# Two ways to take the inverse roots of thirteen RMS norms: square root plus reciprocal, or logarithm plus exponential

## The reference: what is computed

```python
def rms_norm(x, g):
    x32 = x.astype(jnp.float32)
    y = x32 * lax.rsqrt(jnp.mean(x32 * x32, axis=-1, keepdims=True) + RMS_EPS)
    return (y * g.astype(jnp.float32)).astype(x.dtype)
```

## Time and profile before

| | |
|---|---|
| median of three runs | 3220.3 us |
| profiled execution, its own time | 3220.06 us |
| its span (first to last instruction) | 3217.5 us |
| PE busy | 3034.4 us (94%) |
| DVE busy | 1767.5 us (55%) |
| ACT busy | 1015.8 us (32%) |
| mean granted clock of PE | 0.967 |

### The profile page before, as it was taken

How to read it: one execution, slowest core, us unless ns; L and a number is a source line. 1 busy time by engine, 2 the same in 40 slices (tenths; PEclk the granted TensorE clock), 3 DMA queues, 4 the chain that set the end, 5 groups by cost and what they waited for, 6 DMA issues and landing times.

```text
span 3217.5 us, 51830 instructions
## 1 busy us (share of the span) xinstructions
PE 3034.4 (94%) x21724; PEld 2586.9 (80%) x21724; DVE 1767.5 (55%) x3317; ACT 1015.8 (32%) x1745; POOL 222.6 (7%) x455
## 2 busy tenths in 40 slices
PE   8999999999999899999999999989999897789997
PEld 7777998999999887789897888858888464568886
DVE  4564577457566447457755756556356453553334
ACT  4655232332122246523223222233222215332221
POOL 0130222000000102122200000000000000000000
PEclk8989999999999999989999999989999998899998
DMA  5201111235443320111123545312334210122231
GB/s 176 101 15 47 50 67 59 71 135 181 144 137 112 119 79 28 47 45 64 59 80 138 183 145 170 117 49 98 110 114 172 102 32 29 53 70 102 90 100 70
DMA packets 74494, 302.47 MB, mean 94 GB/s; under 512 B 10728, under 2 KB 11112, under 8 KB 69272
## 3 DMA queue, kind: packets, MB, share of 16 engines
q1 hardware_dynamic: 57880, 230.04, 21.1%
q0 software_dynamic: 16384, 69.13, 6.0%
HBM read 288.51 MB, written 14.63 MB: 94 GB/s over the span
## 4 chain that ended last, share of the span: by engine, by line
PE 85%; DVE 7%; ACT 5%; issue 2%; DMA 1%; POOL 0%; ACTq 0%; DVEq 0%; SPq 0%
PE acc L1040 17%; PE acc L1041 17%; PE acc L1042 17%; PE acc L1302 5%; PE acc L1303 5%; PE acc L1304 5%; PE acc L1059 2%; PE acc L1205 2%; ACT temps L1709 1%; PE acc L1074 1%; DVE work L2035 1%; PE acc L1179 1%; PE acc L1533 1%; PE acc L1152 1%; PE acc L1347 1%
## 5 line engine op out<-in xcount | busy, mean ns | idle before, releaser
L1041 PE MATMUL acc<-normed_r,toep_r 128*128 128x512 f32 (+1 forms) x1824 | 642.8, 352 | 0.0
L1638 ACT ACTIVATE toep_r<-ring 128x1024 fp32r<-128x1024 f32 (+2 forms) x340 | 392.6, 1157 | 707.4 <-PE acc L1042 691.1
L2086 DVE TENSOR_TENSOR ring_r<-ring,toep_r 128x1024 fp32r<-128x1024 f32 (+2 forms) x340 | 457.9, 1348 | 261.6 <-ACT toep_r L1638 261.2
L1041 PEld LDWEIGHTS acc<-normed_r,toep_r 128*128 128x128 f32 x1824 | 344.5, 189 | 46.1 <-issue 0.2
L1040 PE MATMUL acc<-mixed_r,toep_r 128*128 128x264 f32 (+1 forms) x1056 | 342.6, 324 | 5.1 <-DVE ring_r L2086 4.4
L1040 PE MATMUL acc<-work_r,toep_r 128*128 128x512 f32 (+1 forms) x988 | 341.7, 346 | 1.5 <-DVE ring_r L2086 1.4
L1042 PE MATMUL acc<-work_r,ring_r 128*128 128x512 f32 (+1 forms) x988 | 340.9, 345 | 0.0
L1042 PE MATMUL acc<-mixed_r,ring_r 128*128 128x264 f32 (+1 forms) x1056 | 338.8, 321 | 0.0
L1040 PE MATMUL acc<-temps_r,toep_r 128*128 128x512 f32 x768 | 305.0, 397 | 24.3 <-DVE normed_r L2072 14.8
L1041 PE MATMUL acc<-work_r,toep_r 128*128 128x512 f32 (+1 forms) x880 | 307.3, 349 | 0.0
L1302 PE MATMUL acc<-residual_r,toep_r 128*128 128x264 f32 (+1 forms) x1024 | 301.8, 295 | 3.7 <-ACT toep L1818 2.1
(11 more groups left out here) (408 smaller groups left out, 5379.3 us busy)
## 6 DMA issues: line engine op xcount, KB each, us to landing
ring<-in_w_pair SPq DMA_DIRECT2D x176, 512.0 KB, 3.5
ring<-in_w_down SPq DMA_DIRECT2D x64, 704.0 KB, 4.1
ring<-in_w_gb SPq DMA_DIRECT2D x64, 640.0 KB, 3.9
extra<-in_w_ada POOLq DMA_DIRECT2D x18, 1024.0 KB, 6.2
toep<-in_w_ada POOLq DMA_DIRECT2D x18, 1024.0 KB, 6.1
ring<-in_w_tm SPq DMA_DIRECT2D x24, 512.0 KB, 4.5
ring<-in_w_out SPq DMA_DIRECT2D x24, 512.0 KB, 3.5
ring<-in_w_fm SPq DMA_DIRECT2D x20, 512.0 KB, 3.8
```

Source lines behind the costliest of these rows:

```text
L1041: mm(out, wh, xl[:, a:z], start=False, stop=False)
L1638: A(high(ld), slot(ld), ACT.Copy).then_inc(S["w_high"], 1)
L2086: V.tensor_tensor(low(ld), slot(ld), high(ld), ALU.subtract).then_inc(S["w_low"], 1)
```

## The change

The reciprocal on VectorE and its semaphore go. `root` takes the logarithm of the mean (with epsilon as bias) and then the exponential of minus half of it, both on ScalarE; the exponential waits for the logarithm through a semaphore of ScalarE's own, and it is the exponential that releases VectorE. A new helper, `log_table`, takes the logarithm of a column of ones, which makes the logarithm's table the one in place, and it waits for its own end in the same way. It stands ahead of the squares of a norm, ahead of the last products of a feed-forward (the second half of the `down` loop), or ahead of the output products of a mixer; `n_ssm` has none.

```diff
             def root(n, rinv_used=None):
                 act.wait_ge(S["sq_used"], n["sq0"] + len(n["tiles"]))
                 if rinv_used:
                     wait(act, rinv_used)
-                A(two(RINV, n["pieces"]), n["acc"], ACT.Sqrt, bias=epsc).then_inc(S["mean_read"], 1)
-
-            def squares(n, rinv_used=None):
+                x = two(RINV, n["pieces"])
+                link(A(x, n["acc"], ACT.Ln, bias=epsc))
+                A(x, x, ACT.Exp, scale=-0.5).then_inc(S["mean_read"], 1)
+
+            chain = [0]
+
+            def link(ins_):
+
+                chain[0] += 1
+                ins_.then_inc(S["scalar_chain"], 1)
+                act.wait_ge(S["scalar_chain"], chain[0])
+
+            def log_table():
+
+                link(A(logc, onecol, ACT.Ln))
+
+            def squares(n, rinv_used=None, ahead=True):
+                if ahead:
+                    log_table()
                 for i in range(len(n["tiles"])):
                     square(n, i)
                 root(n, rinv_used)
...
+                    if half:
+                        log_table()
                     for i, j in enumerate(f["down"][half]):
...
                     high_weights(ly["out"][1].loads[0])
+                    log_table()
                     for i, j in enumerate(ly["out"]):
...
                 squares(b2["n_attn"])
-                squares(b2["n_ssm"], b2["n_attn"]["done"][-1])
+                squares(b2["n_ssm"], b2["n_attn"]["done"][-1], ahead=False)
                 high_tiles(b2["x_out"])
+                log_table()
                 for i, j in enumerate(b2["out"]):
...
             def rinv(n):
                 dve.wait_ge(S["mean_read"], n["n"] + 1)
-                r = two(RINV, n["pieces"])
-                V.reciprocal(r, r).then_inc(S["rinv_ready"], 1)
-                dve.wait_ge(S["rinv_ready"], n["n"] + 1)
                 return n["pieces"][0][0], n["pieces"][-1][1]
```

More of the change, by code:

```diff
@@ L319, in build @@
         ostat = cell(20)
+        logc = cell(1)
         dec = [cell(2) for _ in range(2)]
@@ L448, in build @@
             constants_set start_used lb_shift lb_exp lam_dots lam_exp cact_ready""".split()
-        names += """sq_ready sq_used mean_read rinv_ready stat_ready stat_rooted gate_scaled silu_ready""".split()
+        names += """sq_ready sq_used mean_read stat_ready stat_rooted gate_scaled silu_ready""".split()
         names += """u_ready h_done f_done fm_ready tm_ready gate_ready act_ready
```

## The result

The changed kernel took 3200.62 us (median of 4 runs, 3200.07 to 3202.03), the kernel before in the same timing (a set of runs taken together) 3220.53: ratio 0.9939, 95% interval [0.9922, 0.9956]. The profiled execution has a span of 3198.0 us against 3217.5, so its gain is 19.5.

The account below looks back on a forecast made before the run. TensorE was taken as the bound (85% of the chain of waits), gaining only where it waits for ScalarE and VectorE. Terms 8.7 + 2.45 + 0.6 + 1.5 + 1.9 - 2.3 = 12.85 us gave 3207.2 us, range 3201.5 to 3213.5.

Parts of the forecast that it names:

- The chain's price: At one norm, from the logarithm's start to the first normed tile: 2.66 us in place of 4.11, gain 1.45 us.
- The first norm: Program's first norm: first load ahead of the input, shorter chain, but weight splits on ScalarE behind it; gain 1.5 us.
- The clock's part of the pair: At `n_attn` and `n_ssm`: longer idle time puts the second set of means at the low clock, losing up to 2.7 us.
- The chain of one norm: Clean chains at `pre1`, `post1`, `premix`, `postmix`, `pre2`, `post2`: 1.45 us won at each, 8.7 us together.
- Second layer's first norm: There the square root's load ran late and the logarithm's table is in place long before: gain 2.45 us.
- the feed-forwards: Norms ahead of the two feed-forwards: the SiLU and the split weights come earlier; gains 1.0 and 0.9, together 1.9 us.
- the final norm: Final norm: first normed tile 1.45 us earlier, but ScalarE is late for the squares of `pre1`; gain 0.6 us.
- the early gains are swallowed: Rival: first two layers' gains (5.85 us) go into the next wait for weights or their split; 3213.0 us, chance 0.09.
- the clock gives half of them back: Rival: low-clock stretches end when they ended before, so 5.9 us is given back; 3213.1 us, chance 0.13.
- `n_attn` and `n_ssm` (-2.3): Both norms together: later squares and means, and a second set of means at the low clock; loss 2.3 us.
- I save no such stretch: Behind longer idle times elsewhere: low-clock stretches start and end earlier with the work, so no gain from the clock.

Follow-up runs that it names:

- the two later traces: Traces of the unedited changed kernel, timed twice more: 3206.56 us, ratio 0.9966, and 3203.51 us, ratio 0.9953, to the kernel before.
- the rows with one load and with two: With two: the changed kernel plus a small square root between each logarithm and its exponential, 3222.63 us; with one: the changed kernel, 3200.62 us.
- the three traces: Traces of the same changed kernel from its first timing and two later ones: 3200.62, 3206.56 and 3203.51 us.
- the late load: The changed kernel without the small logarithm ahead of the squares of `n_attn`: 3202.87 us, ratio 0.9951 to the kernel before.
- one activation: The kernel before with the reciprocal square root of the magnitude in place of square root and reciprocal, loads staying where they were: 3170.31 us, ratio 0.9857.

## Why the prediction was right, and where it failed

The chain's price was right. Three steps failed. The first norm was put at 1.5 us and gave 5.70 in the result. The clock's part of the pair was put at -1.9 and gave 0.84 in the result and -0.58 in the two later traces. And at `pre1` the clock was put at nothing and gave 0.9 to 1.0.

- **The chain of one norm (6 x 1.45): right.** 2.66 us as forecast, and 7.45 us for the five behind `pre1`, forecast at 7.25. The prediction let the 1.55 us of `log_table` fit into about 1.4 at `premix` and `pre2`, 0.15 too much by its own numbers; the table shows no loss there. The Trainium skill's page ScalarE: Activation LUTs (What ACT_TABLE_LOAD costs) would have made it an estimated 0.07 us each, by its drain; the rows with one load and with two show no drain. Nor did the page's section Table sets: the hidden batching unit hold here, by which a logarithm followed by an exponential needs one load: all thirteen roots have one between the two.
- **Second layer's first norm, the feed-forwards, the final norm: right**, 2.54, 1.89 and 0.77 against 2.45, 1.9 and 0.6. The SiLU starts 3.97 us after the logarithm (3.96 forecast), and TensorE's wait behind it is 1.17 us in place of 2.16. The two rivals, in which the early gains are swallowed or the clock gives half of them back, fall by the table: up to 1109 us the three traces have won 8.2, 4.9 and 8.2 us, and 4.95 were forecast.

```profile
703.44 0.70 ACT L1624 ACTIVATE work<-acc,small 128x528 f32<-128x528 f32 x1 [6.22 <-PE acc L1090]
...
707.41 0.65 ACT L1708 ACTIVATE work<-work 128x528 f32<-128x528 f32 x1
...
710.41 0.36 PE L1041 MATMUL acc<-mixed_r,toep_r 128*128 128x264 f32 x1 [1.17 <-DVE ring_r L2104]
```

- **The program's first norm (1.5): failed.** Its steps were there: the first square at 5.00 us, TensorE back 0.98 us earlier, another 1.0 while it works at ScalarE's pace, so 2.0 where I took 1.5. The term left out the table that the new exponential leaves behind, which takes a load out 37 us later, 1.2 us of TensorE's wait. That makes 3.2; the three traces stand 2.5 above it, 1.7 below (1.1 of that is the late weight) and 0.8 above. The rest is the clock: the low stretch behind this norm ends at 28.3, 31.6 and 28.4 us where it ended at 33.0 before, and the one from 50.0 to 53.4 us is missing in the result alone. The rows answer to the earlier trace rows:

```profile
0.74 1.28 ACT L1637 ACT_TABLE_LOAD   x1 [0.74 <-PEq L2881]
...
5.00 1.18 ACT L1616 ACTIVATE work<-residual 128x528 f32<-128x528 f32 x2 [2.77 <-DMA residual<-in_x]
5.79 10.27 PE L1090 MATMUL acc<-work,con 128*128 128x264 f32 x32 [5.79 <-ACT work L1616]
...
22.27 5.99 PE L1060 MATMUL acc<-residual_r,temps_r 128*128 128x264 f32 x16 [6.21 <-ACT residual_r L1670]
```

- **`n_attn` and `n_ssm` (-2.3): failed.** All starts were as worked out (the squares 1.65 later, the idle time 3.33), and what the starts cost without the clock, -0.5 to -0.4, is the -0.4 of the forecast. What failed is the clock: I took "as long an idle time, so the same low clock" from one example. The set of means after 3.33 to 3.34 us of idle time took 6.46 us in the kernel before, 3.80 in the result, 5.37 in the second and third traces of the same program, 6.68 with the late load, and 3.80 with one activation. So the loss that I forecast, a second set longer than 3.80 us, is in two traces of the changed kernel (1.57 us) and not in the result. And I left the first set as it was: it got shorter by 0.84 in the result (5.62) and by 0.99 in the other two (5.47). Measured in all: 0.35, -0.99, -0.98.
- **"I save no such stretch": failed at `pre1`.** Its sixteen mean matmuls, 10.28 us before, took 9.29 in the result and 9.40 in the other two, for the stretch of low clock there was 6.8 and not 10.2 us long. That is 0.9 to 1.0 us in all three traces. First the kernel before, then the result:

```profile
2133.09 10.28 PE L1089 MATMUL acc<-work,con 128*128 128x512 f32 x16 [5.86 <-ACT work L1615]
```

```profile
2123.77 9.29 PE L1090 MATMUL acc<-work,con 128*128 128x512 f32 x16 [5.09 <-ACT work L1616]
```

- **The range.** Of the 6.65 us by which the profiled gain missed, 2.65 are the pair, 4.2 the first norm, 1.2 the final norm with `pre1`, 0.3 the other steps, and -1.7 the unchanged stretches. Terms of that size move between executions of one program: the same kernel has gains of 19.5, 11.7 and 15.0 us in three traces, and medians of 3200.6, 3206.6 and 3203.5. The forecast of 3207.2 is near the second by luck: there a stretch without any changed instruction lost 4.2 us and hid gains that I had not foreseen. The range held only what the steps left unknown, not the program's own movement, of which the three times of the kernel before (5 us apart) gave notice.
- **Left open:** why the clock rises after 13.7 us in one execution and after 30.7 in another with the same instructions. No run told what sets it. The second and third timings were made on two different chips, so a part that belongs to the chip isn't told apart either; but single runs of one timing, on one chip, lie up to 10.2 us apart as well.

## What to carry to other kernels

Price the chain, step by step from rows: where no engine covers it, such a sum held to about 0.1 us here. Ask of every instruction that needs a table not only what it loads but what it leaves in place for the next, on a list as long as the program. And before a gain of half a per cent is explained, run the same program again: here that alone moved it between 11 and 20 us, while the version that took the whole reciprocal off the path with one activation (47 us) was beyond doubt at once.

## What the runs showed that I had not expected

- TensorE's granted clock after a wait was no function of the wait's length: 3.34 us of idle time ahead of eight mean matmuls went with 1.2 GHz in one kernel (6.46 us) and with 2.4 GHz in another (3.80 us), and 3.33 us went with 3.80 and with 5.37 us in two executions of one program.
- A low-clock stretch at the same work was 13.7 us long in some traces and 30.7 in others, with 5.4 us between them.
- A second table load with a small dependent activation added 1.52 us to a clean chain (4.18 against 2.66), no more than their lengths; where TensorE's wait grew by it to 2.68 us, the clock fell behind the wait and it cost 4.3.
